# A two-block model on one core: the first block's stages written out in another order

## The reference

```python
mod = silu(c) @ w_ada + b_ada            # 6 x 1024 shifts, scales and gates; also for c_ctx
h  = rmsnorm(x, norm1_g) * (1 + sc_a) + sh_a ;  hc = the same of the 256 context tokens
s_f, s_b = context_states(hc)            # keys, values and decays of the context
q, k, v, g, a_low, p = split(h @ w_in)   # 4 heads; 64-wide keys, 128-wide values
o = gla_bidirectional(q, k, v, la_f, la_b, s_f, s_b)
o = rmsnorm(o) * silu(g);  pooled = pool_mixer(p, w_pool, pool_scale)
x = x + gt_a * (concat([o, pooled]) @ w_out)
h2 = rmsnorm(x, norm2_g) * (1 + sc_m) + sh_m
x = x + gt_m * hier_moe(h2)              # 32 experts, 2 for each token
```

## Time and profile before

| | us |
|---|---|
| median of 3 runs (1254.68 to 1259.27) | 1257.17 |
| the profiled execution | 1263.61 |
| its span in the trace | 1261.8 |
| mean granted clock of TensorE | 0.946 of full |
| busy: TensorE, VectorE, ScalarE | 93%, 53%, 40% of the span |

### The profile page before, as it was taken

The page is one execution under the profiler, slowest core; times in us unless marked ns, Lnnn a source line. Parts: engine busy times, 40 slices in busy tenths (PEclk is TensorE's granted clock), DMA queues, the critical chain, the costliest instruction groups (busy, mean ns, idle before and its releaser), DMA issues.

```text
span 1261.8 us, 19737 instructions
## 1 busy us (share of the span) xinstructions
PE 1171.1 (93%) x8336; PEld 981.7 (78%) x8336; DVE 673.3 (53%) x1055; ACT 498.8 (40%) x763; POOL 0.2 (0%) x4
## 2 busy tenths in 40 slices
PE   5799998789999999689999999799999999999986
PEld 2668877545555554679999987699889999999985
DVE  0825536433333333566655586857655676655566
ACT  2536313311111112353444453235883454443452
POOL 0000000000000000000000000000000000000000
PEclk9899968789999999799999989899999999999988
DMA  9735414699999968155454433232334545455320
GB/s 371 280 135 200 168 67 163 252 411 420 416 412 413 409 252 362 37 195 202 171 197 169 153 125 111 87 135 100 117 118 176 201 167 211 163 196 201 122 80 34
DMA packets 38156, 258.56 MB, mean 205 GB/s; under 512 B 4368, under 2 KB 5008, under 8 KB 7728
## 3 DMA queue, kind: packets, MB, share of 16 engines
q1 hardware_dynamic: 36720, 253.02, 52.7%
q10 hardware_dynamic: 1344, 4.23, 0.8%
HBM read 256.18 MB, written 1.05 MB: 204 GB/s over the span
## 4 chain that ended last, share of the span: by engine, by line
PE 83%; DVE 8%; ACT 5%; issue 2%; DMA 1%; ACTq 0%; DVEq 0%
PE bank L527 82%; DVE wl L1660 1%; DMA xt<-in_x 1%; ACT wh L1158 1%; DVE acc L1712 1%; DVE rstd L1681 1%; DVE xt L1703 1%; ACT arena L1168 0%; PE bank L854 0%; DVE hl L1717 0%; ACT hh L1225 0%; DVE arena L2197 0%; ACT L1168 0%; ACT hh L1229 0%; DVE yl L1677 0%
## 5 line engine op out<-in xcount | busy, mean ns | idle before, releaser
L527 PE MATMUL bank<-hh,wh 128*128 128x256 f32 (+1 forms) x1256 | 368.6, 293 | 6.3 <-DVE hl L1717 6.1
L527 PE MATMUL bank<-hl,wh 128*128 128x256 f32 (+1 forms) x1256 | 362.7, 289 | 0.0
L527 PE MATMUL bank<-hh,wl 128*128 128x256 f32 (+1 forms) x1256 | 362.3, 288 | 0.0
L1660 DVE TENSOR_TENSOR wl<-raw,wh 128x1024 fp32r<-128x1024 f32 (+3 forms) x246 | 278.0, 1168 | 120.4 <-ACT wh L1158 119.2
L1158 ACT ACTIVATE wh<-raw 128x1024 fp32r<-128x1024 f32 (+3 forms) x246 | 236.3, 1005 | 79.4 <-PE bank L527 78.1
L527 PEld LDWEIGHTS bank<-hh,wh 128*128 128x128 f32 x1256 | 246.0, 196 | 13.2 <-issue 10.0
L527 PEld LDWEIGHTS bank<-hl,wh 128*128 128x128 f32 x1256 | 246.1, 196 | 1.9 <-issue 0.8
L527 PEld LDWEIGHTS bank<-hh,wl 128*128 128x128 f32 x1256 | 245.8, 196 | 1.0
L527 PE MATMUL bank<-yh,wh 128*128 128x256 f32 x512 | 146.4, 286 | 7.5 <-DVE yl L1677 5.8
L527 PE MATMUL bank<-yl,wh 128*128 128x256 f32 x512 | 145.8, 285 | 0.0
L527 PE MATMUL bank<-yh,wl 128*128 128x256 f32 x512 | 145.8, 285 | 0.0
(11 more groups left out here) (226 smaller groups left out, 1336.1 us busy)
## 6 DMA issues: line engine op xcount, KB each, us to landing
raw<-in_gu SPq DMA_DIRECT2D x40, 1024.0 KB, 11.1
raw<-in_w_ada SPq DMA_DIRECT2D x24, 1024.0 KB, 7.1
arena<-in_gu SPq DMA_DIRECT2D x24, 1024.0 KB, 10.6
raw<-in_gd SPq DMA_DIRECT2D x22, 1024.0 KB, 9.0
raw<-in_f1g SPq DMA_DIRECT2D x11, 1024.0 KB, 4.9
raw<-in_f2g SPq DMA_DIRECT2D x11, 1024.0 KB, 4.9
raw<-in_f2u SPq DMA_DIRECT2D x11, 1024.0 KB, 4.9
raw<-in_f2d SPq DMA_DIRECT2D x11, 1024.0 KB, 4.8
```

The lines of the kernel that those rows point to most:

```text
L527: return pe.matmul(o, l, m, start=start, stop=stop, skip_group_check=True)
L1660: v.tensor_tensor(WL[slot_of[U]][:, 0:n], src, WH[slot_of[U]][:, 0:n].bitcast(f32), ALU.subtract).then_inc(S("wl"), 1)
```

## The change

- `w_ada` goes in pairs: 12 times `ada_rows(i)` with 16 matmuls into one bank, one copy, and one `turn(i)` of two matmuls with four columns each. It was 24 times 8 matmuls, a copy and a turn.
- The decay input and the keys are one weight (`w1ak`, two chunks of 1536 columns), first in line, with the input blocks outermost: for block x its nine matmuls run once `hx_l` and `hc_l` of that block are there. ACT and DVE modulate both inputs block by block in turn.
- The order of PE behind it: `dec`, p0, p1, pooling, q, v0, `poolw`, v1, the four key transposes together, `ada_rows(4)`, then states and scores, with g0 between the scores of head 1 and the outputs of head 0.
- `w_out` is cut into its pooled rows (`w_op`) and its head rows (`w_og`). Both halves of `w_op` come ahead of both halves of `w_og`.
- The router has the tokens as the stationary operand: 16 matmuls with 36 columns, and no step through `RT`.
- The first ring has four buffers; the fifth holds the pooled values until `yp_l` and joins at g1.
- `through(name)` splits up to the named chunk and no further. It takes the place of `ahead` in this block.

```diff
+        def add_ada(*pairs):
+            for i in pairs:
+                add("w_ada", 2 * i)
+                add("w_ada", 2 * i + 1)
+
+        add_ada(0, 1)
+        add("w1ak", 0)
+        add("w1ak", 1)
+        add_ada(2, 3)
...
+        add_ada(4, 5)
+        add("w1g", 0)
+        add_ada(6)
+        add("w1g", 1)
+        add_ada(7, 8)
+        add("w_op", 0)
+        add_ada(9)
+        add("w_op", 1)
+        add("w_og", 0)
+        add("w_og", 1)
+        add_ada(10)
         add("w_r", 0)
-        add("w_ada", 23)
+        add_ada(11)
...
+        eaten = list(range(len(chunks)))
+        late = where["w1ak", 0]
+        eaten[late:late + 6] = [late + 4, late + 5, late, late + 1, late + 2, late + 3]
+
+        def units_used(U):
+            return 2 * eaten[U // 2] + U % 2 + 1
...
+        ring = collections.deque(range(NR - 1))
         for c in range(len(chunks)):
+            if c == where["w1g", 1]:
+                ring.appendleft(NR - 1)
...
+            def ada_rows(i):
+                b = take(pe, ("ada", i))
+                ws = []
+                for c in (2 * i, 2 * i + 1):
+                    arrived(pe, where["w_ada", c])
+                    ws.append(RAW[raw_of[where["w_ada", c]]][:, :].rearrange("p (k n) -> p k n", k=8))
+                for u in range(4):
+                    for c in range(2):
+                        for k in range(2):
+                            p = 64 * c + 32 * k
+                            t = mm(b[p:p + 32, 0:256], CV[:, 2 * u + k, :], ws[c][:, 2 * u + k, :], u == 0, u == 3)
+                t.then_inc(S("used"), 4)
 
...
+            turn(2)
+            turn(3)
+
+            ba, bk = take(pe, ("a", 0)), [take(pe, ("k", m)) for m in range(2)]
+            for i in range(2):
+                for u in range(2):
+                    h, l = weights(2 * where["w1ak", i] + u, 2)
+                    for k in range(2):
+                        x = 4 * i + 2 * u + k
+                        pe.wait_ge(*nth("hx_l", x + 1))
+                        pe.wait_ge(*nth("hc_l", x + 1))
+                        for m, o in enumerate([ba] + bk):
+                            f = slice(m * 128, m * 128 + 128)
+                            t = mm3(o[:, :], h[:, k, f], l[:, k, f], HW[:, x, :], LW[:, x, :], x == 0, x == 7)
+                            if x == 7 and m == 0:
+                                t.then_inc(S("a_mm"), 1)
+                    t.then_inc(S("used"), 1)
+            pe.wait_ge(*nth("d_g", 48))
+            evicted(pe, ("a", 0))
+            for j in range(4):
+                b = take(pe, ("dec", j))
+                mm(b[:, :], WDEC3[0:32, j // 2, (j % 2) * 128:(j % 2) * 128 + 128], ASB[0:32, :], True, True).then_inc(S("dec"), 1)
+            lin_tm(("w1p", 0), [take(pe, ("p", 0))], 2, HX, LX)
             lin_tm(("w1p", 1), [take(pe, ("p", 1))], 2, HX, LX)
-            ada_rows(9)
-            lin_fm(("w1a", 0), [take(pe, ("a", 0))], HW, LW, ("hc_l", up), ncols=128, N=512)
             pe.wait_ge(*nth("d_a0", 32))
...
-            ada_rows(10)
+            lin_fm(("w1q", 0), [take(pe, "q")], HX, LX)
+            lin_tm(("w1v", 0), [take(pe, ("v", 0, 0)), take(pe, ("v", 0, 1))], 4, HW, LW)
             for gq in range(2):
                 b = take(pe, ("poolw", gq))
...
+            def mix_out(name, n, outs, xs, last):
+                ws = [weights(2 * where[name, n] + u, 2) for u in range(2)]
+                for m in range(4):
+                    o, head = outs[m]
+                    for x in xs:
+                        if m == 0:
+                            if x % 2 == 0:
+                                pe.wait_ge(*nth("yo_l" if last else "yp_l", x % 4 // 2 + 1))
+                        h, l = ws[x % 4 // 2]
+                        f = slice(m * 128, m * 128 + 128)
+                        t = mm3(o, h[:, x % 2, f], l[:, x % 2, f], YH[:, x, :], YL[:, x, :], head and x == 0, last and x == 7)
+                    if last and m < 3 and (n or m == 1):
+                        t.then_inc(S("wo_mm"), 1)
+                t.then_inc(S("used"), 2)
+
+            def out_banks(n):
...
+            for j in range(4):
+                turn_keys(j)
+            ada_rows(4)
             states(0)
             scores(0)
-            ada_rows(16)
+            turn(4)
+            ada_rows(5)
             states(2)
             scores(1)
-            ada_rows(17)
+            turn(5)
+            lin_fm(("w1g", 0), [take(pe, ("g", 0))], HX, LX)
             outs(0)
             states(1)
             scores(2)
-            ada_rows(18)
+            ada_rows(6)
             outs(1)
+            turn(6)
             states(3)
             scores(3)
             lin_fm(("w1g", 1), [take(pe, ("g", 1))], HX, LX)
+            outs(2)
             head_norm(0)
-            outs(2)
-            ada_rows(19)
+            ada_rows(7)
             outs(3)
+            turn(7)
+            ada_rows(8)
             head_norm(1)
-            turn(19)
-
-            for i in range(4):
-                b = take(pe, ("wo", i))
-                if i == 0:
-                    pe.wait_ge(*nth("yp_l", 2))
-                lin_fm(("w_out", i), [b], YH, YL, ("yo_l", [0, 0, 0, 0, 1, 1, 2, 2]) if i == 0 else None)
+            turn(8)
+            wo0 = out_banks(0)
+            mix_out("w_op", 0, wo0, range(4), False)
+            ada_rows(9)
+            wo1 = out_banks(1)
+            mix_out("w_op", 1, wo1, range(4), False)
+            turn(9)
+            mix_out("w_og", 0, wo0, range(4, 8), True)
+            mix_out("w_og", 1, wo1, range(4, 8), True)
...
+            ada_rows(10)
+            b = take(pe, "router")
             arrived(pe, where["w_r", 0])
-            w = RAW[raw_of[where["w_r", 0]]][:, 0:512].rearrange("p (k n) -> p k n", k=8)
+            w = RAW[raw_of[where["w_r", 0]]][:, 0:288].rearrange("p (k n) -> p k n", k=8)
             for k in range(8):
                 pe.wait_ge(*nth("n2_h", k + 1))
-                t = mm(b[64 * (k % 2):64 * (k % 2) + 64, 0:256], w[:, k, :], H2F[:, k, :], k < 2, k >= 6)
+                for x in range(2):
+                    t = mm(b[:, 256 * x:256 * x + 36], H2F[:, k, 128 * x:128 * x + 128], w[:, k, :], k == 0 and x == 0, k == 7)
             t.then_inc(S("used"), 2)
             for x in range(2):
                 for q in range(2):
@@ -754,13 +778,7 @@
...
+            def through(name, i=0):
+                split_to(2 * where[name, i] + 1)
+
+            def ada_row(i):
+                done(a, "w_ada", 2 * i + 1)
+                if i >= 2:
+                    a.wait_ge(*nth("turn", i - 1))
+                copy_out(("ada", i), ROW[i % 2], bank(("ada", i))[:, 0:256])
 
...
             a.wait_ge(*nth("mod1", 4))
             for k in range(8):
                 a.activation(HX[:, k, :], XN[:, k, :], ACT.Identity, scale=A1[:, 0, k:k + 1], bias=B1[:, 0, k:k + 1]).then_inc(S("hx_h"), 1)
-            ahead("w1p", 0)
-            a.wait_ge(*nth("cn", 4))
-            for k in range(8):
+                if k == 0:
+                    a.wait_ge(*nth("cn", 4))
+                if k >= 2:
+                    a.wait_ge(*nth("hc_l", k - 1))
+                a.activation(SQ[k % 2][:, :], CT[:, k, :], ACT.Identity, scale=A1[:, 1, k:k + 1], bias=B1[:, 1, k:k + 1]).then_inc(S("tnc"), 1)
...
+            through("w1q")
+            for i in range(2):
+                done(a, "w1p", i)
+                copy_out(("p", i), PTM[:, :, i * 256:i * 256 + 256], two(bank(("p", i))))
+                if i == 0:
+                    through("w1v", 0)
...
             decay_exps(0)
+            for gq in range(2):
+                a.wait_ge(*nth("pool", gq + 1))
+                copy_out(("pool", gq), PY[:, 2 * gq:2 * gq + 2, :], two(bank(("pool", gq))))
+            done(a, "w1q")
+            copy_out("q", QS, two(bank("q")))
+            decay_exps(1)
+            through("w1v", 1)
+            decay_exps(2)
             values_in(0)
-            decay_exps(1)
-            ada_row(13)
-            decay_exps(2)
-            keys_out(0)
+            decay_exps(3)
+            for gq in range(2):
+                evicted(a, ("poolw", gq))
+                a.activation(YH[:, 2 * gq:2 * gq + 2, :], PY[:, 2 * gq:2 * gq + 2, :], ACT.Copy).then_inc(S("yp_h"), 1)
+            through("w1g", 0)
             values_in(1)
-            decay_exps(3)
-            keys_out(1)
-            ada_row(14)
-            keys_out(2)
-            lin("w1g", 0)
-            copy_out(("g", 0), GS[:, 0:2, :], two(bank(("g", 0))), ACT.Silu)
-            keys_out(3)
+            for j in range(4):
+                keys_out(j)
...
             head_gate(0)
+            through("w_op", 0)
             head_out(2)
-            ada_row(19)
+            ada_row(7)
             head_out(3)
             head_gate(1)
+            ada_row(8)
+            through("w_op", 1)
+            ada_row(9)
+            through("w_og", 0)
+            through("w_og", 1)
...
```

(65 more changed lines are left out.)

363 lines of the change are left out of this document (139 added, 224 removed).

## The result

The changed kernel takes 1271.93 us (median of 4 runs, 1270.74 to 1272.70), the kernel before 1258.22 beside it (1254.68 to 1262.04): a ratio of 1.0108, interval 1.0076 to 1.0139, so 13.7 us slower. Predicted were 1275 and a range of 1254 to 1287. The profiled execution after took 1272.70, its span is 1270.9.

A forecast was written before the change was run, and what follows sets the result against it. PE bounds the kernel, with waits and 1.2 GHz stretches beside its matmuls; the unchanged gather onward passes on any shift. Terms summed to +17.3 us, put on the median 1257.2: 1274.5, said as 1275, range 1254 to 1287.

The forecast's parts named there:

- Front: Until shifts and scales are there: w_ada 6 and 7 queue behind the w1ak splits; +1 to +3.4, taken as +2.0 us.
- Modulation: Under the first block's matmuls: ACT and DVE steps and a half-clock start against 4.6 us lost before; -0.3 us.
- Pooling waits for ACT: Behind the last dec: ACT needs 14.7 us before p1 is out, PE has 11.5 us of matmuls; +3.2 us.
- v0: Its split on DVE now stands behind decay_apply(0), which needs q out of its bank; +3.1 us.
- g0: Its load is issued only after ada_rows(4), its split precedes the copies the states wait for; PE stands +10.0 us.
- The clock behind it: After the g0 wait: PE stays at 1.2 GHz through sparse matmuls into g0; bounds 0 and 11.8, taken as +11.8 us.
- Outputs of the heads: Head outputs: g0's dense matmuls right ahead may hold the clock longer; bounds -9 and +1, taken as -1.5 us.
- Second head norm: turn(8) waits 6.7 us for a row ACT copies behind the whole gate, so w_op stands too; net +4.6 us.
- Tail: From w_out's last matmul to the gather: shorter statistic wait, earlier router; bounds -5 and -9.7, taken as -6.5 us.
- rival 1: Clock returns in the sparse stretch ahead of g0, taking 11.8 off: +5.5, or 1263 us; chance 0.12.
- the prediction's own sign: Wrong if the g0 load is issued well ahead of the transposes' end, or the clock is 1.00 behind that wait.
- The waits that go and the turns: Waits before head norms, for copies and at first key transposes vanish, -5.2 us; six turns saved behind the front, -2.8.

The follow-up runs named there:

- the router's place: Kernel before with the token-stationary router, w_r and the router also moved ahead of w_ada 21 to 23: 1258.72 us, ratio 0.9984.
- the four cures: Changed kernel with early w1g 0 load, rows 7 and 8 copied inside gates, values' stage reordered, front reordered with later w1ak splits: 1236.44 us, ratio 0.9803.

## Why the prediction was right, and where not

The sign held, the places of the waits too, and most of their sizes, and the time lies in the range. That it lies 3 us from the 1275 is in part luck. The sum made against the trace was +17.3, and the traces differ by 9.1 (1270.9 less 1261.8): 8.2 too much. The medians differ by 13.7. I put the difference between two executions on a median of three runs, 6.4 under the profiled execution (1263.61), and this took back most of the excess. With all 79 executions of the kernel before the median is 1261.90, and the profiled one lies only 1.7 above it.

| step of the prediction | predicted | measured |
|---|---|---|
| Front | +2.0 (to +3.4) | +5.7 |
| Modulation | -0.3 | +0.7 (2.3 to the first matmul, 6.0 at 0.50: 3.0 lost, less 4.6) |
| Pooling waits for ACT | +3.2 | 1.4 here; 1.5 and 1.6 in two more traces, 2.9 to 3.0 in five |
| Slow stretch after `dec` | -3.1 | -3.0 (3.5 at 0.52: 1.7 lost instead of 4.7) |
| v0 | +3.1 | 3.4 |
| g0 | +10.0 | 10.3 |
| The clock behind it | +11.8 | 1.7 (3.3 at 0.50) |
| Outputs of the heads, clock | -1.5 | -7.0 (12.8 at 0.50: 6.4 lost instead of 13.4) |
| `turn(7)` | +2 | 2.9 |
| Second head norm (wait) | 6.7 | 6.67 |
| Tail | -6.5 | -9.2 |

*The clock behind it* is the step that failed, and its failure is one of choice: I had the bounds 0 and 11.8 and took the upper "by the nearest row". That row, 21.3 us at 0.50, was not the nearest. It begins as the first head's outputs end; the states and scores before it, the very work that now stands behind the wait, ran at 1.00 from 142.8 to 151.7 in the same group. The kernel without the narrow matmuls and the one with them spread out, one trace each, show no fall there: these matmuls in a row are what brings the clock down. Behind the wait, seven traces give 3.2 to 11.6 us at 0.50, 1.6 to 5.8 lost; the predicted 23.7 at 0.50 was never seen. This is the mechanism of rival 1, given 0.12, and by the prediction's own sign (a clock of 1.00 there) the step was wrong. That the time still isn't rival 1's 1263 is made up by what the sum had too small or not at all: the front, v1 and the half-clock starts. The rule of the Trainium skill that I set beside it ("TensorE: Matmul & The Clock Gate", "What's actually happening": open while kept busy) agrees with that return. It doesn't agree with the fall: PE is busy 7.60 of 7.60 us ahead of the one at 179.20 (171.60 to 179.20), and in the 9.50 us behind it as well; there the kind of matmul decides, as those two kernels show.

*Outputs of the heads*: mis-sized. The 13.4 that before lost was one execution's. With the same work up to there, the trace of the kernel before with the router alone has 20.4 us at 0.50 from 153.9, and that with the router's place two stretches of 3.3 and 3.4, where before has 26.8. A term read from one trace's slow clock carries this spread of 10 us.

*Front*: mis-sized, by its load. The two rows of after (SP's issues, then PE's pair):

```profile
36.39 2.06 SPq L2432 DMA_DIRECT2D raw<-in_w_ada  x2
...
45.15 3.64 PE L516 MATMUL bank<-raw,arena 128*32 128x256 f32 x32 [6.86 <-DMA raw<-in_w_ada]
```

The two loads behind the splits were issued from 36.4, as predicted, but PE started on them at 45.15, 8.8 after the first issue, not 4.8. Two chunks are under way together, with those of p issued behind from 38.50; that they share the time is likely, but no run separates it. The kernel with the front's order changed shows that the order is the cause of 3.7 of the 5.7 (shifts at 47.0).

*Tail*: near its upper bound, since the router ran half at the higher clock (5.12 instead of the 7.4 in the sum). The kernels before with the router show that this is not its form: by itself it gains nothing. By their traces, of the 9.2 some 3.9 are form and place together, 2.4 the statistic's shorter wait (1.0 against 3.36) and 1.9 the router's clock (5.12 against 7.01); 1.0 is left.

*v1* was missed, 2.1: most likely a bank that DVE empties only behind `decay_apply(3)`. I followed what PE needs as an operand, not the bank that it writes. For *v0* the parts named in the prediction add up to 3.75 at most, not 3.1; it measured 3.4.

The waits that go and the turns, -8.0 together, weren't tested singly; the waits are absent from after's view. With these, the second head norm (+4.6), the half-clock starts behind v0 and v1 (1.4 each), the wait for v1 and the start of `w_op` (5.7 at 0.50, 2.8 lost), the sum up to the gather is 11.2; the traces show 11.5.

## What to carry to other kernels

When a change reorders the use of weights, go through each load and ask on which release it is issued, and what the engine that unpacks it must do before it may do anything else; here one line's place cost 13 us, and two copies of 0.4 us behind a reciprocal 9. The reordered kernel lost, and with four such places mended it beats the kernel before by some 2% (ratio 0.980, 0.976 to 0.984): a slower result may lie in the schedule around an idea, not in the idea. Don't take a term from the slow clock of a single trace; look at what kind of work each slow row begins in, and take a second trace where the term decides.

## What the runs showed of the hardware

The clock's stretches at 0.50 differ between executions of one program: 3.3, 3.5 and 11.6 us behind the same wait. It falls as a head's outputs end, most of which are matmuls of 64 columns in a row, though PE counts as busy throughout: at 155.8 in before (they begin at 151.74), at 168.3 and 179.2 in after (164.11, 174.53), at 150.6 with the four cures (146.69). Not every row of them brings it down: the first head's, from 137.91 with the four cures, doesn't. It stays at 1.00 from 122 to 189 us when the same matmuls are spread among dense ones. But there they cost more than in a row, 1.4 us for the head spread in g0 and 2.8 for the one in pair 6, and this takes more than the clock gives.
